# Down stages with 7 and 8 of 22 squares per pass in seven products, and six weight lows per layer made by accumulating transfers

## The reference

```
u = h @ w_up                     # 256x2048 @ 2048x11264
u = causal depthwise conv, width 3, + bias
gate, val = split(u)
out = (silu(gate) * val) @ w_down   # 256x5632 @ 5632x2048
```

## Time and profile before

| | us |
|---|---|
| median of 3 runs | 2487.33 |
| lowest and highest | 2486.79, 2487.71 |
| the profiled execution's own time | 2487.73 |
| its span, first to last instruction | 2485.9 |

### The profile page before, as it was taken

One profiled execution on the slowest core, in us unless ns is written; L12 is line 12 of the kernel. 1 busy time (PEld: TensorE's weight loads), 2 busy tenths in 40 slices (PEclk: granted clock), 3 DMA queues, 4 the chain that ended last, 5 costly groups with the idle time before them and its releaser, 6 DMA issues.

```text
span 2485.9 us, 29114 instructions
## 1 busy us (share of the span) xinstructions
PE 2477.3 (100%) x11403; PEld 2061.0 (83%) x11403; DVE 2162.0 (87%) x2389; ACT 1472.0 (59%) x1436; POOL 44.3 (2%) x54
## 2 busy tenths in 40 slices
PE   9999999999999999999999999999999999999999
PEld 8888788888888888888888888888888888888887
DVE  7888867999999999998778878876699999999998
ACT  6555645766667666556545545544576676756654
POOL 1000000000000000000000000000000000000000
PEclk9999999999999999999999999999999999999999
DMA  8555554767676656577555666654476776755754
GB/s 284 195 187 170 169 186 147 228 202 248 191 251 205 208 187 215 178 238 201 158 156 170 195 198 187 189 169 155 139 249 203 232 217 204 233 185 199 244 172 159
DMA packets 359401, 491.24 MB, mean 198 GB/s; under 512 B 20005, under 2 KB 200437, under 8 KB 356832
## 3 DMA queue, kind: packets, MB, share of 16 engines
q1 hardware_dynamic: 355024, 465.64, 57.1%
q0 software_dynamic: 4000, 23.63, 4.4%
q10 hardware_dynamic: 240, 0.10, 0.0%
HBM read 468.31 MB, written 3.68 MB: 190 GB/s over the span
## 4 chain that ended last, share of the span: by engine, by line
PE 93%; DVE 4%; ACT 1%; DMA 1%; issue 1%; ACTq 0%; SPq 0%
PE psum L2073 47%; PE psum L2077 24%; PE psum L1923 5%; PE psum L1914 5%; PE psum L1915 5%; PE psum L2176 2%; PE psum L2303 1%; DVE w_lo L1143 1%; PE psum L1872 0%; DVE w_lo L1151 0%; PE psum L2267 0%; PE psum L2301 0%; PE psum L2275 0%; ACT w_hi L684 0%; DMA w_raw<-in_f_w_up 0%
## 5 line engine op out<-in xcount | busy, mean ns | idle before, releaser
L2073 PE MATMUL psum<-w_hi,xT 128*128 128x512 f32 x4456 | 1115.0, 391 | 0.0
L2073 PEld LDWEIGHTS psum<-w_hi,xT 128*128 128x128 f32 x4456 | 833.3, 188 | 171.5 <-issue 0.2
L671 ACT ACTIVATE w_hi<-w_raw 128x2048 fp32r<-128x2048 f32 (+1 forms) x350 | 631.3, 1810 | 390.6 <-PE psum L2077 258.3
L1143 DVE TENSOR_TENSOR w_lo<-w_raw,w_hi 128x2048 fp32r<-128x2048 f32 (+1 forms) x332 | 704.9, 2145 | 55.3 <-ACT w_hi L671 54.7
L2077 PE MATMUL psum<-w_lo,xT 128*128 128x512 f32 x2228 | 583.9, 389 | 1.1 <-DVE w_lo L1151 0.9
L2077 PEld LDWEIGHTS psum<-w_lo,xT 128*128 128x128 f32 x2228 | 417.8, 188 | 89.6 <-DVE w_lo L1151 2.2
L1151 DVE TENSOR_TENSOR w_lo<-w_raw,w_hi 128x2048 fp32r<-128x2048 f32 (+1 forms) x174 | 375.8, 2176 | 49.8 <-ACT w_hi L684 49.4
L684 ACT ACTIVATE w_hi<-w_raw 128x2048 fp32r<-128x2048 f32 (+1 forms) x174 | 315.7, 1827 | 154.2 <-PE psum L2077 68.1
L2073 PE MATMUL psum<-w_hi,mixT 128*128 128x512 f32 x992 | 265.3, 389 | 0.0
L1914 PE MATMUL psum<-w_hi,xT 128*128 128x512 f32 x624 | 245.1, 393 | 1.0 <-DVE phase L1296 1.0
L1915 PE MATMUL psum<-w_hi,xT 128*128 128x512 f32 x624 | 243.1, 390 | 0.0
(11 more groups left out here) (203 smaller groups left out, 1795.1 us busy)
## 6 DMA issues: line engine op xcount, KB each, us to landing
w_raw<-in_f_w_up SPq DMA_DIRECT2D x352, 512.0 KB, 5.1
w_raw<-in_f_w_down SPq DMA_DIRECT2D x176, 512.0 KB, 5.2
w_raw<-in_b_w_qkv SPq DMA_DIRECT2D x192, 256.0 KB, 3.8
w_raw<-in_a_w_qkv SPq DMA_DIRECT2D x132, 256.0 KB, 5.1
w_raw<-in_b_w_qkv SPq DMA_DIRECT2D x256, 128.0 KB, 2.7
w_lo<-w_raw POOLq DMA_DIRECT2D x18, 1024.0 KB, 7.1
w_raw<-in_a_w_o SPq DMA_DIRECT2D x16, 1024.0 KB, 5.2
w_raw<-in_b_w_qkv SPq DMA_DIRECT2D x32, 512.0 KB, 6.1
```

The costliest lines, as they stand in the source:

```text
L671: nc.scalar.activation(w_hi[:, slot, cols], w_raw[:, slot, cols], ACT.Copy).then_inc(hi_ready, 1)
L1143: nc.vector.tensor_tensor(w_lo[:, slot, cols], w_raw[:, slot, cols], w_hi[:, slot, cols], ALU.subtract).then_inc(lo_ready, 1)
L2073: pe.matmul(o, x[:, h, P * m:P * (m + 1)], hi, start=start and h == 0, stop=False)
```

## The change

It replaces the form of the two passes. Pass 0 had 6 plain squares and groups of 2, 2, 3, 3, 2, 3; it gets 5 and groups of 3, 2, 2, 2, 2, 2, 3. Pass 1 had 3 and groups of 3, 2, 2, 3, 3, 2, 3; it gets 3 and groups of 3, 2, 2, 2, 2, 2, 2, 3. In each case one last plain square ends the pass. There are thus 7 and 8 squares in seven products per pass instead of 6 and 7, and 59 entries per layer instead of 57. And it names entries whose low is made by transfer: pair 1 of pass 0, pair 0 of pass 1, and the plain square behind the "one" of each group of 3. Counted through, these are entries 1, 6, 25, 29, 33 and 55 of each layer: six per layer, twelve in the program. Entry e+4 of each is one that is loaded (5, 10, 29, 33, 37, and the first of the next stage), never a "sum".

```diff
 UP_BY_DMA = (2,)
-DOWN_BY_DMA = ()
+DOWN_GROUPS = ((5, (3, 2, 2, 2, 2, 2, 3)), (3, (3, 2, 2, 2, 2, 2, 2, 3)))
 PAIRS, HALVES = FB // 2, 2
 ...
-DOWN_ENTRIES = [(what, p, j) for p, form in enumerate(((6, (2, 2, 3, 3, 2, 3)), (3, (3, 2, 2, 3, 3, 2, 3)))) for what, j in down_pass(*form)]
+DOWN_ENTRIES = [(what, p, j) for p, form in enumerate(DOWN_GROUPS) for what, j in down_pass(*form)]
+DOWN_BY_DMA = tuple(e for e, (what, p, j) in enumerate(DOWN_ENTRIES) if (what, p, j) in (("std", 0, 1), ("std", 1, 0))
+                    or DOWN_ENTRIES[e - 1][0] == "one" and DOWN_ENTRIES[e + 2][0] == "std")
```

## The result

The changed kernel takes 2529.89 us (median of four runs, 2527.82 to 2531.07) against 2487.52 of the kernel before beside it (2486.79 to 2487.92). The ratio is 1.017, 95% interval 1.0152 to 1.0187: 42 us or 1.7% slower. The forecast was 2504, with 2518 as its upper end. The direction was right; of the loss only two fifths were foreseen.

The account below looks back on a forecast made before the run. PE, never stopping in the down stage, was taken as the bound. Per layer, waits of 1.1+5.1+2.8+0.8 = 9.8 us less 1.36 give 8.4; 16.9 for two layers on 2487.73 led to 2504 us, range 2492 to 2518.

Parts of the forecast that it names:

- matmuls saved: On PE, two squares per layer go from 24 to 21 matmuls, saving 1.36 us per layer, 2.72 for both.
- runs' pace, both passes: In runs of groups of 2, PE waits 1.25 us per group once DVE's lead is gone: 5.1 and 2.8 us.
- entry 6's landing: Pass 0, entry 6: the transferred low lands at 910.0, needed at 908.9, so PE waits 1.1 us per layer.
- entries 25 and 55: Transferred lows behind a "one" land at t+6.1, needed at t+5.7: PE waits 0.4 us twice per layer, 0.8 in sum.
- entries 1, 29, 33: Transferred lows at these entries land before their use, so PE waits for none of them: cost 0.
- Bound by PE, DVE at its limit in groups of 2: Down stage: PE never stops; a group of 2 takes DVE 11.45 us against PE's 10.20, costing 1.25 of lead.
- The rival in which DVE's smaller sum makes all well: DVE's work falls by 1.4 us per layer, PE never waits and the gain stays: 2484.6 us; chance 0.11.
- the transfer lands 7.1 us later: A transferred low lands 7.1 us after POOL issues it, never under 6.9; for entry 6 that is at 910.0.
- transfers crowd each other: Landings at the trace's longest, 8.6 us for lows and 9.1 for loads: 17 us lost per layer, 2521; chance 0.12.
- DVE idles 3.2 us, and the split falls in the next group: Pass 0: chunk 10's late load idles DVE 3.2 us, activation splits fall at entries 11 and 12; lead about 0 at 12.
- The sum ended with the last entry: Waits were summed only up to entry 55's own landing, 9.8 us per layer, with the second layer assumed to behave alike.
- the forecast's own proviso on landings over 9 us: Entries 29 and 33: three plain squares keep landings 2 to 3 us early; this cover goes if landings take over 9 us.

## Why the prediction missed

**Step by step.** In us per layer, the first layer's stage measured:

| term of the forecast | forecast | measured |
|---|---|---|
| matmuls saved | -1.36 | -1.36 |
| runs' pace, both passes | 5.1 + 2.8 | 7.2 |
| entry 6's landing | 1.1 | 2.0 |
| entries 25 and 55 | 0.8 | 3.4 |
| entries 1, 29, 33 | 0 | 0.8 |
| splits behind a late load | 0 | 5.3 |
| last combination, with the clock behind it | 0 | 5.2 |

- *Bound by PE, DVE at its limit in groups of 2: right.* The period of 11.45 and most stops at 1.12 to 1.16 are in every run with the new squares in which DVE's own work in a group was left alone. The sum, 7.2 for 7.9, is in part luck: pass 0 had three stops and 3.1 us where four and 5.1 were forecast, since PE's own stop at entry 9 gave DVE lead, and pass 1 had four and 4.1 where 2.8 were forecast. The rival in which DVE's smaller sum makes all well is refuted by the changed kernel itself: DVE's sum is smaller, and it is waited for. As forecast, an average of busy time says nothing here.
- *The step "the transfer lands 7.1 us later" failed.* It was read from the earlier trace rows, the transfers of the up stage. In the down stage they landed after 8.1 to 10.2. With the measured landings the forecast's own sums would have been near: entry 6 at 8.1 gives 2.1 (measured 2.0), entries 25 and 55 at 8.6 and 8.8 give 1.9 and 2.1 (measured 1.7 twice). The rival "transfers crowd each other" had the right size of landing, and with its 8.6 gave 2521; its price, too, lacked the terms below. Its mechanism, as named, is not what happened: with entries 1 and 29 alone, some 113 us apart, the landings were as long, 9.0 to 9.9. They are long in this stage however few there are. While the changed kernel's first six were in flight, the queue engines were busy at 0.84 to 1.03; for the nine of the up stage before it was 0.67 to 0.78. That points at the loads beside them (four chunks' loads are issued between 984 and 991, ahead of entry 29's, which took 10.2), but it is argued from rows only, and one row does not fit it: a transfer of the up stage of the changed kernel (616.36) took 9.1 us at a share of 0.59, with no load issued in the 6 us ahead of it. The share forecast for the whole stage, 0.78, did not come (0.64), and would have said nothing.
- *The step "DVE idles 3.2 us, and the split falls in the next group" failed.* I saw both the late low of chunk 10 and the split behind it, and charged both to DVE's lead at the runs. But this split belongs to a block that PE needs at entry 9, before any run. The chain above takes 20.3 us from the transfer's issue (901.85) to PE's start at 922.18, and the stop is direct, 2.12 us; the run without entry 6 shows it. At entries 31 and 36 a split is late as well, behind loads that took 13.5 and 9.3 us beside a transfer. All three went when the split was moved ahead.
- *The sum ended with the last entry: that failed.* Behind entry 55's transfer wait the next stage's first load, its high, its low on DVE, and in DVE's order the last combination. PE waits 3.4 us for it and the granted clock of the window behind the stop is 0.83, a mean between its two levels of 1.2 and 2.4 GHz; before the stop PE had been busy at 1.00. The second layer has nothing behind it and lacks this term; that is most of the 6 us between the layers, which I had taken for alike. The clock had no term in the forecast at all, and took 1.8 us here and 1.7 in the second layer.
- *Costs at nothing: right for entries 1 and 29* when they stand alone, though their landings took 9 us and more; in company entry 29 waits 0.8, as the forecast's own proviso on landings over 9 us had it. Entry 33 landed in time, but the load beside it did not.

What stays open: how much of the longer landings is due to loads rather than to something else in this stage. No run moved the loads alone.

## What to carry to other kernels

When work moves from a loaded engine to a queue, follow the landing to everything behind it: who reuses the buffer, whose load that releases, and which unrelated instruction stands behind that load's consumer in an in-order engine, over the stage's end too. Take a transfer's landing time from a stretch that is as full of loads as the one it goes to, and if the slack is below the spread of those rows, count it as exposed. Look also at what the transfer does to the loads in flight beside it. And give a stop of 2 us or more a price beyond its length: where the clock fell behind one here, it cost 1.7 us or more again. And where an engine keeps pace only with the help of spare time between dense groups, compare its period with the bound's period group by group: five dense groups in a row cost what no average shows.

## What the chip showed beside this

- A transfer of 1 MB that adds within the chip's buffers landed after 6.9 to 8.6 us in the up stages of the kernel before (6.9 to 9.1 in those of the changed kernel) and after 8.1 to 11.0 in the down stages. Half the bytes took 5.1 to 7.4, not half the time. The Trainium skill, "DMA: Bandwidth & Descriptors", section "Anatomy of one DMA — SWDGE (gpsimd) path", gives about 2.0 us and the bytes at 436 GB/s, by which 512 KB is estimated at 3.2 us and 1 MB at 4.4; the rows are at about twice either, and the difference of 2.4 between the sizes is twice its 1.2.
- Loads of 512 KB reached 13.5 us in the changed kernel's stage, against 9.1 in the earlier trace rows.
- GpSimd's additions and subtractions of 128x128 had medians of 0.79 to 2.38 us by line where DVE takes 0.28 (spans on GpSimd are rough), and DVE's instructions beside them were 7 to 20% longer; with a later start of the sums that cost four fifths of what moving them off DVE had freed.
- The granted clock was 0.83 in the window 1120 to 1130, behind a stop of PE of 3.4 us, and again in 2320 to 2330, around one of 2.3; in the windows with stops of 0.8 to 2.1 us between 900 and 990 it was 1.00. Over the runs the length of the stop alone does not tell which it will be: it stayed at 1.00 behind stops of 2.12 us (changed kernel, 922.18) and 2.27 (activations' lows by transfer, 952.48), and was 0.83 in the window with a stop of 2.05 (without entry 55, 910.90) and of 1.96 (without entry 6, 2413.22).
